# Group-norm variances in four column groups of one bank, with the factors spread by one-row products

## The reference

```
o = o.swapaxes(0, 1).reshape(bn, L, RET_HEADS, RET_DV)
mu = jnp.mean(o, -1, keepdims=True)
var = jnp.mean(jnp.square(o - mu), -1, keepdims=True)
o = ((o - mu) * lax.rsqrt(var + LN_EPS)).reshape(bn, L, RET_WIDTH) * gn_g + gn_b
return jax.nn.silu(g) * o, s_new
...
mix = jnp.concatenate([ya, yb, yc], axis=-1).astype(x.dtype) @ p['w_out']
x = layer_norm(ALPHA * x + mix, p['ln1_g'], p['ln1_b'])
```

## Time and profile before

| | |
|---|---|
| median of 3 timed runs | 672.84 us |
| span of the profiled execution | 671.2 us |
| median less that span | 1.6 us |
| PE busy | 661.3 us, 99% |
| DVE busy | 560.6 us, 84% |
| ACT busy | 417.7 us, 62% |
| chain that ended last, by engine | PE 90%, DVE 6%, ACT 2% |

### The profile page before, as it was taken

One profiled execution on the slowest core, in us unless ns is written; L12 is line 12 of the kernel. 1 busy time (PEld: TensorE's weight loads), 2 busy tenths in 40 slices (PEclk: granted clock), 3 DMA queues, 4 the chain that ended last, 5 costly groups with the idle time before them and its releaser, 6 DMA issues.

```text
span 671.2 us, 13446 instructions
## 1 busy us (share of the span) xinstructions
PE 661.3 (99%) x5048; PEld 614.0 (91%) x5048; DVE 560.6 (84%) x1121; ACT 417.7 (62%) x694; POOL 134.6 (20%) x158
## 2 busy tenths in 40 slices
PE   8999999999999999999999999999999999999997
PEld 6777887989999999999977788989999999999996
DVE  6988979989998988789488998798999898884753
ACT  5776258767676666645746546786767666663343
POOL 0070420150222222200226400106022222220011
PEclk9999999999999999999999999999999999999999
DMA  8776530747674655554356463454766555556511
GB/s 326 248 261 216 201 128 1 288 107 224 212 250 155 209 178 179 202 189 153 131 181 228 159 210 130 131 204 152 204 215 195 183 181 195 173 188 193 161 56 65
DMA packets 42916, 121.82 MB, mean 181 GB/s; under 512 B 5539, under 2 KB 15171, under 8 KB 42339
## 3 DMA queue, kind: packets, MB, share of 16 engines
q1 hardware_dynamic: 40466, 115.22, 51.3%
q0 software_dynamic: 1088, 4.11, 2.5%
q10 hardware_dynamic: 1296, 1.63, 0.7%
HBM read 115.33 MB, written 5.61 MB: 180 GB/s over the span
## 4 chain that ended last, share of the span: by engine, by line
PE 90%; DVE 6%; ACT 2%; issue 1%; DMA 1%; SPq 0%; DVEq 0%; ACTq 0%
PE ps L448 21%; PE ps L449 20%; PE ps L450 20%; PE ps L441 14%; PE ps L512 2%; DVE z L1513 1%; DVE z L1521 1%; DMA z<-in_xT 1%; PE ps L460 1%; PE ps L461 1%; PE ps L462 1%; PE ps L563 1%; PE ps L575 1%; PE ps L745 1%; PE ps L797 1%
## 5 line engine op out<-in xcount | busy, mean ns | idle before, releaser
L1609 DVE TENSOR_TENSOR w_lo<-ring,w_hi 128x1024 fp32r<-128x1024 f32 x144 | 175.4, 1220 | 31.2 <-ACT w_hi L983 29.4
L448 PE MATMUL ps<-x_hi,w_hi 128*128 128x264 f32 x672 | 191.0, 284 | 1.0 <-DVE x_lo L1559 1.0
L449 PE MATMUL ps<-x_lo,w_hi 128*128 128x264 f32 x672 | 190.4, 283 | 0.0
L450 PE MATMUL ps<-x_hi,w_lo 128*128 128x264 f32 x672 | 190.3, 283 | 0.0
L983 ACT CAST w_hi<-ring 128x1024 fp32r<-128x1024 f32 x144 | 150.2, 1043 | 60.0 <-PE ps L450 58.9
L448 PEld LDWEIGHTS ps<-x_hi,w_hi 128*128 128x128 f32 x672 | 126.5, 188 | 1.9 <-issue 1.8
L449 PEld LDWEIGHTS ps<-x_lo,w_hi 128*128 128x128 f32 x672 | 126.6, 188 | 0.0
L450 PEld LDWEIGHTS ps<-x_hi,w_lo 128*128 128x128 f32 x672 | 126.0, 187 | 0.0
L441 PE MATMUL ps<-x,ring 128*128 128x264 f32 x448 | 104.7, 390 | 0.3 <-ACT x L1059 0.3
L448 PE MATMUL ps<-hff_hi,w_hi 128*128 128x264 f32 x352 | 100.0, 284 | 0.0
L450 PE MATMUL ps<-hff_hi,w_lo 128*128 128x264 f32 x352 | 99.9, 284 | 0.0
(11 more groups left out here) (364 smaller groups left out, 1148.9 us busy)
## 6 DMA issues: line engine op xcount, KB each, us to landing
ring<-in_units SPq DMA_DIRECT2D x187, 512.0 KB, 3.6
kv<-in_kpool SPq DMA_DIRECT2D x32, 128.0 KB, 2.7
kv<-in_vpool SPq DMA_DIRECT2D x32, 128.0 KB, 2.4
SR<-in_sret SPq DMA_DIRECT2D x2, 1024.0 KB, 6.2
out_rsample<-SR POOLq DMA_DIRECT2D x2, 1024.0 KB, 5.2
out_kv<-hb ACTq DMA_DIRECT2D x2, 528.0 KB, 4.5
VBC<-v_rows POOLq DMA_DIRECT2D x8, 128.0 KB, 3.9
out_y<-x SPq DMA_DIRECT2D x3, 264.0 KB, 2.0
```

What stands on the lines that cost most here:

```text
L448: mm(out, wh, hi, start=start, stop=False)
L449: mm(out, wh, lo, start=False, stop=False)
L450: return mm(out, wl, hi, start=False, stop=stop)
L1609: E.did(tt(w_lo[:, slot], ring[:, ring_slot(L * UNITS + i)], w_hi[:, slot].bitcast(F32), ALU.subtract), "w_lo")
```

## The change

The variances are written by four products with 32 columns of the constant matrix, each into its own 32 partitions of bank 4 (tile positions 0, 32, 64, 96), so one bank holds all four heads, 32 equal rows each. ACT's logarithm and exponential run once over 264 columns, and `rg` is one tile of 264 columns. A new function, `gn_spread`, stands on PE between the retention state and the output projection: four products, each with one row of ones as the weight and one row of `rg` (partition 32h) as the moving operand, into banks 4 to 7, which puts a head's factor on all 128 partitions. DVE's scaling reads the factor there, in PSUM, and waits for the second count of `gvar`, which the last of these four products gives.

```
-        rg = turn[:, 0]
+        rg = turn[:, 0, 0]
...
-                "gvar": 4, "gv1": 1, "gr": 1, "gsil": 2,
+                "gvar": 2, "gv1": 1, "gr": 1, "gsil": 2,
...
             def gn_vars(L):
+
+                bank = claim(4, "gv1", L, 1)
                 for h in range(HEADS):
                     pe.wait_ge(S("gsq"), HEADS * L + (1 if CENTRED[L] else h + 1))
-                    bank = claim(4 + h, "gv1", L, 1)
-                    E.did(mm(bank[:, 0:T], C["mean_v"], sqo[:, h], start=True, stop=True), "gvar")
+                    ins = mm(bank[32 * h:32 * h + 32, 0:T], C["mean_v"][:, 0:32], sqo[:, h], start=True, stop=True,
+                             tile_position=(0, 32 * h))
+                E.did(ins, "gvar")
+
+            def gn_spread(L):
+
+                need(pe, "gr", L, 1)
+                for h in range(HEADS):
+                    bank = claim(4 + h, "catc", L, h + 1)
+                    ins = mm(bank[:, 0:T], C["ones"][32 * h:32 * h + 1], rg[32 * h:32 * h + 1], start=True, stop=True)
+                E.did(ins, "gvar")
...
                 ret_state(L)
+                gn_spread(L)
...
                     if i == at_["gvar"]:
-                        need(act, "gvar", L, HEADS)
-                        E.did(f(rg[:], ps[:, 4:8, 0:T], ACT.Ln, bias=eps_t[LN_EPS]), "gv1")
+                        need(act, "gvar", L, 1)
+                        E.did(f(rg[:], ps[:, 4, 0:T], ACT.Ln, bias=eps_t[LN_EPS]), "gv1")
...
             def gn_scale(L, h):
-                need(dve, "gr", L, 1)
-                E.did(stt(Oh[:, h], Oh[:, h], pv(L, "gn_g", h), rg[:, h], ALU.mult, ALU.mult))
+                need(dve, "gvar", L, 2)
+                E.did(stt(Oh[:, h], Oh[:, h], pv(L, "gn_g", h), ps[:, 4 + h, 0:T], ALU.mult, ALU.mult))
```

## The result

The changed kernel takes 677.52 us, the median of 4 runs (676.73 to 677.66), against 672.9 us of the kernel before, the median of 4 runs (672.66 to 673.32) beside it: a ratio of 1.0063, 95% interval 1.0049 to 1.0077. A second set of runs of the same program gave 676.75 us (4 runs) against 672.68 (21 runs), ratio 1.0058 (1.0043 to 1.0074). So the loss is 4.1 to 4.6 us; 3.2 were predicted.

The account below looks back on a forecast made before the run. PE bounds the kernel, with DVE's chain deciding at the group norms. Scaling delays of 1.87 us (layer 0) and 1.34 (layer 1) sum to 3.2; span 671.2 becomes 674.4, plus 1.6 gives 676.0 us, range 674.2 to 677.6.

Parts of the forecast that it names:

- What bounds the place: Around both group norms, DVE's ordered work behind the first scaling sets PE's loss; ACT's gain reaches nothing PE waits for.
- The set of four variances: On PE, column groups take 0.66 us instead of 1.78, gaining 0.49 us in layer 0 and 1.02 in layer 1.
- The spread: Four one-row products on PE behind the retention state, 0.73 us to their end; DVE's first scaling waits for the last.
- no overlap: Rival: product sets do not overlap on PE, scaling 3.58 us late per layer; 680.0 us, or 678 if one fails; 7%.
- The delays: DVE's first scaling starts 1.87 us late in layer 0 and 1.34 in layer 1, both passing on to PE.
- ACT: Logarithm and exponential on 264 columns take 0.515 and 0.423 us, gaining 1.3 us per layer that PE never sees.
- Faster through ACT: Rival: layer 1's chain through the variances and ACT shrinks by 2.3 us, giving 670.5 us; 5%.
- covered: Rival: the scaling's wait is hidden, only PE's own work counts, about zero change, 672.9 us; 10%.
- PE's waits: PE waits about 1 us before the first output product for DVE's low part, and in layer 0 also before L472.
- Half absorbed: Rival: layer 0's delay is won back from PE's other idle time, only layer 1's 1.34 us counts, 674.2 us; 4%.
- no later place had a time of its own: From L472 on everything hangs on PE and DVE, so the delay cannot vanish in any later place.
- nothing in the program runs to a clock of its own: Argument against layer 0's delay being won back from PE's 9.9 us of idle time over the span.

Follow-up runs that it names:

- the reordered kernels: Changed kernel with the spread ahead of the retention state: 674.45 us; with DVE's low parts 0 to 3 ahead of all four scalings: 673.76; with both: 673.11.

## Why the prediction was right, and where its size was off

- **What bounds the place**: right. DVE's order behind the scaling, not ACT and not PE's own work, sets the loss; the reordered kernels took it away step by step, at 674.45, 673.76 and 673.11 us (for 676.75).
- **The set of four variances**: predicted 0.66 us to the next start, gain 1.02 us in layer 1. Measured 0.59 (437.36 to 437.95) against 1.58 before (434.37 to 435.95), 0.99. That 1.02 came so close is in part luck: it took 1.78 us from layer 0 for the set before, 0.20 too much for layer 1, and 0.76 with the switch for the new set, 0.17 too much. In layer 0 the gain was 113.34 - (113.88 - 1.18) = 0.64 for 0.49.
- **The spread**: 0.73 us to its end as taken from the row groups of the earlier trace rows; one-row operands overlap just as well. The rival "no overlap" is out.
- **The delays**: 1.87 and 1.34 us predicted, 1.84 and 1.39 measured; DVE is idle for 1.77 us in layer 0 and, in the two profiles of the changed kernel, for 2.09 and 1.48 in layer 1, about the 1.5 to 2 that were named. Reading the scaling's factor in PSUM cost nothing (0.49 us as before).
- **ACT**: 0.46 and 0.42 us for 0.515 and 0.423, hidden as said.
- **"Faster through ACT" and "covered"**: the kernel without the spread shows what the shorter chain alone is worth: 0.1 us in the medians (672.56 for 672.68), 1.1 at most by its interval, and 0.53 us in layer 1 by the trace. The prediction allowed 0.21 us there, the time for which DVE waits ahead of that scaling in its one trace; in the second profile of the kernel before DVE waits 0.77 us. Cover there is, but only once the order on both engines is changed.
- **PE's waits**: about 1 us before the first output product, as said (1.05); the second one, before L472 in layer 0, is small, since PE waited for low parts in between too and comes there late itself: 0.31 us from 129.48 to 129.79, where the same step took 0.12 before (126.79 to 126.91).
- **"Half absorbed"**: layer 0's delay reached layer 1 almost whole (1.71 of 1.84).
- **The step that failed** is the sentence that no later place had a time of its own, and "nothing in the program runs to a clock of its own". The ring load of layer 1 lands late beside an instruction fetch, whose place moved when PE instructions were added: 0.42 us in the first profile, 0.76 in the second. With it the sum is 3.2 + 0.4 to 0.8, some 3.6 to 4.0 us, against 4.1 measured with the second set. In the first set, 4.6 us, the remaining half microsecond is left open; its profiled execution had the chance late start of 1.18 us.

## What to carry to other kernels

An engine that works in order makes everything behind a waiting instruction wait too: before adding a wait, look at what is queued behind it and needs nothing from it, and put that ahead. Making a stage shorter is worth only what the chain through it gains; here ACT saved 2.2 us and PE 1.6 at the variances, and a wait put behind two other pieces of PE's work turned that into a loss. When a small change costs half a microsecond in a place that it does not touch, look at the transfers there, instruction packets too, before explaining it by the edit.

## What the runs showed that was not expected

- A 512 KB load with one 16 KB instruction packet beside it landed 1.2 to 2.3 us later (4.71 for 3.5, 5.7 for 3.4), and PE lost 0.4 to 1.5 us; which load it was changed with the number of PE instructions that stood ahead.
- With 24 tiny products in place of two idle ones of 264 columns, PE still ran at half its pace at 9 us, where it had reached its full pace at 5 us; the record of the full clock begins at 12.48 us instead of 5.01. The 1.00 that a profile gives for stretches ahead of its first record says nothing of the clock there.
